# A two-block decoder stack on one Trainium2 core: shared keys projected once, rotary keys beside the latents, the merge in another order

## The reference, cut to what matters

```python
q = q_a.reshape(B, S, G, HPG, dh).transpose(0, 2, 3, 1, 4)          # G = 2 groups, HPG = 4 heads
k_cmp, v_cmp, k_slc, v_slc, k_win, v_win = [z.reshape(B, S, G, dh) for z in jnp.split(kv_a, 6, axis=-1)]
kc = _compress(k_cmp, pe_k, ck_w1, ck_w2)                           # blocks of 32 tokens, stride 16
vc = _compress(v_cmp, pe_v, cv_w1, cv_w2)
...
o_a = _nsa(q_a, kv_a, g_a, ...)      # compressed, selected and window attention, gated per head
o_b = _swa_sink(q_b, k_b, v_b, ...)  # window of 128, 2 groups, a sink
o_c = _fox(q_c, k_c, v_c, f_c, b_f)  # 8 heads with keys of their own, forgetting
merged = g[:, :, 0] * (o_a @ w_br_a) + g[:, :, 1] * (o_b @ w_br_b) + g[:, :, 2] * (o_c @ w_br_c)
return merged @ w_out
```

```python
c_q, c_kv, k_r, hq, hf, hi, hgate, mq, gate_logits = split_sizes(u @ w_in[l], IN_SPLITS)
k_rope = apply_rope(k_r, cos, sin)   # 32 wide, one for all 8 heads
ckv = rmsnorm(c_kv, kv_norm_g)
```

## Time and profile before

| | us |
|---|---|
| median of 3 runs | 2781.98 |
| lowest, highest | 2779.66, 2785.36 |
| the profiled execution, its own time | 2779.37 |
| its span from first to last instruction | 2777.3 |
| TensorE matmuls busy | 2729.1 (98%) |
| GpSimd busy | 2068.5 (74%) |
| ACT busy | 1300.9 (47%) |
| DVE busy | 857.4 (31%) |
| mean granted TensorE clock | 0.997 |

### The profile page before, as it was taken

One profiled execution on the slowest core, in us unless ns is written; L12 is line 12 of the kernel. 1 busy time (PEld: TensorE's weight loads), 2 busy tenths in 40 slices (PEclk: granted clock), 3 DMA queues, 4 the chain that ended last, 5 costly groups with the idle time before them and its releaser, 6 DMA issues. The chain is left out here.

```text
span 2777.3 us, 46964 instructions
## 1 busy us (share of the span) xinstructions
PE 2729.1 (98%) x19086; PEld 2516.8 (91%) x19086; DVE 857.4 (31%) x1473; ACT 1300.9 (47%) x1882; POOL 2068.5 (74%) x920
## 2 busy tenths in 40 slices
PE   8999999999999999999999999999999999999998
PEld 6999899899899989989899899988989989999898
DVE  2633264112224144311211323632121132263212
ACT  4454555444444555444444444644444444464443
POOL 7888566888988945788798774378879877437886
PEclk9999999999999999999999999999999999999999
DMA  6556533555665643755565554255556555425554
GB/s 229 183 190 210 169 122 130 196 184 181 211 191 185 202 150 115 189 191 189 174 208 184 174 177 158 84 176 188 189 167 211 189 169 181 160 84 175 181 185 143
DMA packets 131325, 484.13 MB, mean 174 GB/s; under 512 B 14720, under 2 KB 14720, under 8 KB 130112
## 3 DMA queue, kind: packets, MB, share of 16 engines
q1 hardware_dynamic: 127296, 463.53, 50.2%
q0 software_dynamic: 3840, 17.81, 2.2%
HBM read 478.65 MB, written 2.62 MB: 173 GB/s over the span
## 5 line engine op out<-in xcount | busy, mean ns | idle before, releaser
L1005 POOL TENSOR_TENSOR rest<-ring,upper 128x1024 fp32r<-128x1024 f32 (+2 forms) x848 | 2028.6, 2412 | 639.6 <-ACT upper L1775 620.7
L1775 ACT ACTIVATE upper<-ring 128x1024 fp32r<-128x1024 f32 (+2 forms) x848 | 884.0, 1052 | 775.0 <-DMA ring<-in_weights 773.5
L362 PE MATMUL psA<-xT_upper,upper 128*128 128x256 f32 x2944 | 411.1, 282 | 2.2 <-ACT arena L1775 2.2
L362 PE MATMUL psA<-xT_rest,upper 128*128 128x256 f32 x2944 | 413.1, 283 | 0.0
L362 PE MATMUL psA<-xT_upper,rest 128*128 128x256 f32 x2944 | 405.5, 280 | 0.0
L362 PEld LDWEIGHTS psA<-xT_upper,upper 128*128 128x128 f32 x2944 | 384.3, 189 | 16.0 <-ACT arena L1775 3.5
L362 PEld LDWEIGHTS psA<-xT_rest,upper 128*128 128x128 f32 x2944 | 379.7, 192 | 0.0
L362 PEld LDWEIGHTS psA<-xT_upper,rest 128*128 128x128 f32 x2944 | 372.8, 189 | 0.0
L1245 DVE TENSOR_TENSOR psA<-sil,psA 128x256 f32<-128x256 f32 x144 | 61.8, 429 | 954.3 <-ACT sil L1775 954.2
L362 PE MATMUL psY<-upper,hT_rest 128*128 128x512 f32 x704 | 205.3, 397 | 0.0
L362 PE MATMUL psY<-upper,hT_upper 128*128 128x512 f32 x704 | 203.8, 394 | 0.0
(11 more groups left out here) (258 smaller groups left out, 3185.8 us busy)
## 6 DMA issues: line engine op xcount, KB each, us to landing
ring<-in_weights SPq DMA_DIRECT2D x880, 512.0 KB, 3.3
G<-in_rows POOLq DMA_DIRECT2D x6, 1024.0 KB, 6.5
G<-in_rows POOLq DMA_DIRECT2D x7, 512.0 KB, 6.4
arena<-rel_by_distance POOLq DMA_DIRECT2D x8, 256.0 KB, 13.1
x<-in_x SPq DMA_DIRECT2D x2, 512.0 KB, 5.8
par<-in_params POOLq DMA_DIRECT2D x4, 256.0 KB, 5.8
xn<-in_mem POOLq DMA_DIRECT2D x1, 1024.0 KB, 9.6
memory_transposed<-arena POOLq DMA_DIRECT2D x1, 1024.0 KB, 5.8
```

What stands on the lines that cost most here:

```text
L362: i = pe.matmul(out, lhsT, rhs, start=start, stop=stop)
L1005: pool.tensor_tensor(rest[:, r, 0:n], ring[:, r, 0:n], upper[:, r, 0:n], ALU.subtract)\
L1775: act.activation(out, in_, func, **kw).then_inc(*up)
```

## The change

**Block 2's shared keys.** Heads are renumbered so that a pair of neighbours has one head of each group (`by_pairs` on the weights of `qa`, `qb`, the small gates, sinks, bias tables and branch outputs). Heads on partitions 0 to 63 are then of group 0 and those on 64 to 127 of group 1, and keys need not be doubled. `ks` and `kw` share one bank, `kc` and `vc` another, `kb` takes half a bank: five pieces and not ten. `Z2` gets its two halves by four copies for `k` and four for `v`, all out of the one bank. The two empty pieces are gone too: 213 pieces.

**Block 1's rotary keys.** They stand behind the latents as 64 more columns (704). DVE copies them out of banks Y2 and Y3, doubled, into `rotary`; ACT's squares of those banks wait for that; TensorE turns them into T0 after `mq`. 218 pieces.

**The merge.** `MERGE` gives a new order of the twelve products: (0,0), (0,1), (1,0), (0,2), (1,1), (1,2) and then as before. The third goes to bank Y2. The first is issued before the merge, in block 2 inside step 14 of attention, in block 1 behind attention. The last branch is turned before the third product. ACT splits further ahead around that place.

```diff
-PIECES = 220
+PIECES = (218, 213)
...
-WIDTHS = [_FFN + [PIECE] * 8 + [640] * 8 + [PIECE] * 26 + [0] * 6 + [PIECE] * 40 + _FFN,
-          _FFN + [PIECE] * 22 + [960] * 4 + [PIECE] * 8 + [0, PIECE] * 8 + [PIECE] * 16 + [0] * 2 + [PIECE] * 20 + _FFN]
+WIDTHS = [_FFN + [PIECE] * 8 + [704] * 8 + [PIECE] * 24 + [0] * 6 + [PIECE] * 40 + _FFN,
+          _FFN + [PIECE] * 17 + [960] * 4 + [PIECE] * 8 + [0, PIECE] * 8 + [PIECE] * 36 + _FFN]
...
+MERGE = [(0, 0), (0, 1), (1, 0), (0, 2), (1, 1), (1, 2)] + [(n, br) for n in range(2, 4) for br in range(3)]
...
+            def branch_product(i):
+
+                n, br = MERGE[i]
+                if n == 0:
+                    for t in range(TT):
+                        pe.wait_ge(*taken(("ot", BRANCHES[second()][br], t)))
+                s = shaped(piece(), PIECE, "p (k c) -> p k c", k=4)
+                lab = ("wo", br, n)
+                out = fill(pe, ("A0", "A1", "Y2")[i] if i < 3 else next_a(), lab)
...
             def merge(norm):
 
...
+                last = BRANCHES[second()][2]
+                for i in range(1, 12):
+                    if i == 2:
+                        turn_o(last, lambda qt: taken(("o", last, 0 if last == "mem" else 1, qt)))
+                    branch_product(i)
...
-                by_features("kr", 1)
                 by_features("mq", 2)
+                pe.wait_ge(*sig["rotary copied"].after(1))
+                turn("T0", ("kr", 0), [rotary[:, t, 64 * z:64 * z + P] for z in range(2) for t in range(TT)])
...
-                for n in ("ks", "kw", "kc", "vc"):
-                    by_features(n, 1)
+                by_features("ks kw", 1)
+                by_features("kc vc", 1)
                 by_features("qb", 2)
-                by_features("kb", 1)
+                lab = ("kb", 0)
+                s = shaped(piece(), PIECE, "p (k c) -> p k c", k=KD)
+                by_parts(fill(pe, next_a(), lab)[:, 0:S], s, filled(lab))
+                free()
...
-                           12: lambda: turn_o("swa", lambda qt: taken(("o", "swa", 1, qt)))}, opening)
-                for _ in range(2):
-                    piece()
-                    free()
+                           12: lambda: turn_o("swa", lambda qt: taken(("o", "swa", 1, qt))),
+                           14: lambda: branch_product(0)}, opening)
                 merge(norm + 2)
...
+                for t in range(TT):
+                    lab = ("c", 2 + t)
+                    dve.wait_ge(*full(lab))
+                    dve.tensor_copy(rotary[:, t, 64:192].rearrange("p (z d c) -> p z d c", z=2, d=2),
+                                    at(lab)[:, 256:320].rearrange("p (z c) -> p z c", z=2).unsqueeze(2)
+                                    .broadcast_to([P, 2, 2, 32])).then_inc(*sig["rotary copied"].up(t))
...
+                def pairs_of(at_column, ready):
+
+                    lab = ("kc vc", 0)
+                    dve.wait_ge(*ready)
+                    src = at(lab)[:, at_column:at_column + S]
+                    for g in range(2):
+                        v = src[64 * g:64 * g + 64]
+                        dve.tensor_copy(Z2[0:64, g, :], v).then_inc(*sig["vector step"].up())
+                        i = dve.tensor_copy(Z2[64:128, g, 0:S - 1], v[:, 1:S])
+                        i.then_inc(*(read(lab) if at_column and g else sig["vector step"].up()))
...
+                kept(("ks kw", 0), KSW)
+                pairs_of(0, full(("kc vc", 0)))
+                own()
+                blocks_of("k", par[:, 24:40])
+                pairs_of(S, sig["blocks"].after("k"))
+                dve.wait_ge(*full(("kb", 0)))
+                dve.tensor_copy(KB, at(("kb", 0))[:, 0:S]).then_inc(*read(("kb", 0)))
...
+def by_pairs(w, n):
+
+    return w.reshape(-1, 2, 4, n).transpose(0, 2, 1, 3).reshape(-1, 8 * n)
```

More of the change, by code:

```diff
@@ L305, in base, with pieces_here, after_mix @@
         def base():
-            return layer() * PIECES
+            n = layer()
+            return min(n, DEPTH) * PIECES[0] + max(n - DEPTH, 0) * PIECES[1]
+        def pieces_here():
+            return PIECES[second()]
+        def after_mix():
+            return pieces_here() - FFN_PIECES
         def steps_here():
@@ L659, in turn_o @@
                     turn(f"T{qt}", ("ot", name, qt), [O[:, qt, j * P:(j + 1) * P] for j in range(4)], ready(qt))
-            def merge(norm):
[L663 to L678, removed]
-                        free()
+            def branch_product(i):
[6 more added lines that the diff above has]
+                out = fill(pe, ("A0", "A1", "Y2")[i] if i < 3 else next_a(), lab)
+                for j in range(2):
+                    for w, v, first, last in passes():
+                        for k in range(4):
+                            mm(out[:, j * S:(j + 1) * S], s[w][:, k, j * P:(j + 1) * P], turned_parts[v][:, br, k],
+                               first and k == 0, last and k == 3, filled(lab) if last and j == 1 and k == 3 else None)
+                free()
+            def merge(norm):
+                last = BRANCHES[second()][2]
[3 more added lines that the diff above has]
+                    branch_product(i)
                 y = ("y", norm)
@@ new lines, in merge @@
+                added = {}
+                for n, br in MERGE:
+                    lab = ("wo", br, n)
+                    dve.wait_ge(*full(lab))
+                    src = at(lab).rearrange("p (j c) -> p j c", j=2)
+                    g = G[:, 8 * br + 2 * n:8 * br + 2 * n + 2, :]
+                    if br == 0:
+                        dve.wait_ge(*(taken(("ot", BRANCHES[second()][2], n)) if n < 2 else sig["merged parts"].after(n - 2)))
+                        stt_(sums_of(n), g, 1.0, src, ALU.add, ALU.mult).then_inc(*read(lab))
+                        if n > 1:
+                            rest_of(n - 1)
+                        continue
+                    tmp = (sil[:, :, :], xn[:, 0, 0:512].rearrange("p (a b) -> p a b", a=2))[br - 1]
+                    stt_(tmp, g, 1.0, src, ALU.add, ALU.mult).then_inc(*read(lab))
+                    dve.wait_ge(*taken(("wo", 0, n)))
+                    dve.wait_ge(*taken(lab))
+                    if br == 2:
+                        dve.wait_ge(*sig["vector step"].value(added[n]))
+                        tt_(sums_of(n), tmp, sums_of(n), ALU.add).then_inc(*sig["merged"].up(n))
+                    else:
+                        tt_(sums_of(n), tmp, sums_of(n), ALU.add).then_inc(*sig["vector step"].up())
+                        added[n] = sig["vector step"].count
+                    if (n, br) == (1, 1):
+                        rest_of(0)
@@ L1700, in block2 @@
                 dve.wait_ge(*full(("cmp", "k", 1)))
-                for g in range(2):
-                    zz = Z2[:, g, :]
-                    src = bass.AP(zz.tensor, zz.offset, [zz.ap[0], (2, 16), (16, 15)])
-                    i = tt_(ZB[:, :, 15 * g:15 * g + 15], src, par[:, 40:56].unsqueeze(2).broadcast_to([P, 16, 15]), ALU.add)
-                    i.then_inc(*(sig["blocks"].up("v") if g else sig["vector step"].up()))
+                dve.wait_ge(*taken(("kc vc", 0)))
+                blocks_of("v", par[:, 40:56])
                 lab = ("cmp out", "k")
@@ L2074, in block2 @@
                 for n in range(2):
-                    copy(("qf", n), QF[:, 2 * n:2 * n + 2, :], piece=93 + 2 * n)
-                until(99)
+                    copy(("qf", n), QF[:, 2 * n:2 * n + 2, :], piece=88 + 2 * n)
+                until(94)
                 for z in ("k", "v"):
```

174 lines of the change are left out of this document (69 added, 105 removed).

## The result

The changed kernel takes 2749.25 us (median of 4 runs, 2746.73 to 2751.27) against 2782.53 (4 runs beside it). The ratio is 0.987, with a 95% interval of 0.985 to 0.989. The forecast was 2746, with a range of 2738 to 2755. The profiled execution took 2751.27 us, 28.1 less than that of before; the forecast on that scale was 34.7 less.

A forecast was written before the change was run, and what follows sets the result against it. TensorE's own matmuls were taken to bound the kernel nearly everywhere. Removed matmuls, small additions, new and shortened waits summed to -34.7 us, 2747.3 against the 2782.0 median; the forecast was 2746, range 2738 to 2755.

The forecast's parts named there:

- Bound and price: Nearly everywhere TensorE's own matmuls set the end; a 256-column matmul costs 118.9 ns, a weight piece 2.85 us.
- rival that needed GpSimd or the ring as a bound: Shortened sections: GpSimd bounds next, 2752, chance 0.07; a wait for the ring in the projections would disprove the forecast.
- Rotary keys: Block 1: `kr` pieces gone, -11.4 us; wider latents +2.7, four added transposes a layer +0.8, all for two layers.
- The wait at A1: Block 2's `kc vc` bank: TensorE waits for vector-engine copies and additions, +4.8 us for two layers, bounds 0 to +8.1.
- Rival A: Block 2's `kc vc` bank: additions find GpSimd idle, the bank is free in time, no wait; 2741, chance 0.10.
- Rival C: Block 2's bank A1: the wait is long in both layers and the clock falls at both; 2753, chance 0.10.
- The `kb` bank: Block 2's projections: the copy TensorE waits for shrinks from 512 to 256 columns, -0.5 us in all.
- The merge: End of block 2's attention: the first branch product fills the 1.28 us `PT` wait, -2.6 us in all.
- the two new waits: Block 2, A1: waits of some 2.4 us may each bring a clock dip, +0 to +3.4 us, carried in the range.
- block 1's new order: Block 1's merge: no TensorE wait there today, so worth nothing and costing 0, at most +0.5 us a layer.
- Rivals D and E: Block 2: early product's piece comes late, 2753, chance 0.04; clock stays low after A1's wait, up to 2828, chance 0.01.
- The flag of 20 us at 0.5: Whole run: the forecast is wrong if the granted clock is at 0.5 for over 20 us in all.

The follow-up runs named there:

- e1: The changed kernel again with no edit, for another profile: 2747.47 us (6 runs), ratio 0.987.
- e2: The changed kernel with the old merge order, no early product and block 2's two unread pieces back: 2752.74 us (6 runs), ratio 0.989.
- e3: The kernel before with only the new merge, the two unread pieces gone: 2777.10 us (12 runs), ratio 0.997.
- e8: The changed kernel with block 2's first branch product behind attention, not in step 14, new order kept: 2755.27 us (6 runs), ratio 0.9885.
- e10: The kernel before with no edit, one more execution for another profile: 2795.05 us, mean granted clock 0.991.

## Why the prediction was right, point by point

- **Bound and price.** TensorE's list of matmuls set the time, and 2.85 us a piece held in every profile with the clock at full speed. 14 pieces gave 39.9 us less as worked out; no rival that needed GpSimd or the ring as a bound came up.
- **Rotary keys.** -10.7 and +2.6 us against -10.6 and +2.7. Nothing waits for the copies or the transposes. ACT's squares were covered as said. But the term had no place for the waits of block 1 that come with this part, for `hT_rest` and for `rest` in the second merge: some 1.8 and 0.9 us by the comparison of profiles under e1.
- **The wait at A1.** Right mechanism, right place, right bounds; the term was mis-sized, 2.4 in this profile and 2.0 in the mean where the sum had 4.8. Rival A, no wait at all, had 0.10 and is what two of the seven profiles showed in both layers. Rival C's fall of the clock behind the wait came in two of fourteen layers.
- **The `kb` bank.** 1.05 to 0.72 us a layer, -0.7 against -0.5.
- **The merge.** The `PT` hole closed as said, -3.0 against -2.6. But the term was mis-sized: by the times of e2, e3 and e8 the new merge is worth 5 to 8 us. The step that failed is the one that priced the hole of 1.28 us at its length alone. I carried the clock only for the two new waits, and did not ask what this wait does to it today: in 5 of 12 cases it is followed by 10.2 us at 0.5. The one profile of before that I had showed full speed there, and its own time was below the median. That block 1's new order costs nothing is not contradicted: its wait for `rest` is there with the old order too.
- **Rivals D and E.** The early product's piece was there in time: TensorE starts it at 1792.98, 0.36 us after the start of the transposes ahead of it, and the longest low stretch in any profile of the changed kernel was 6.8 us outside the program's end.
- **The flag of 20 us at 0.5.** It was set without counting the kernel before, whose own profile has 20.5 us of it (with the 6.8 us at the very end, where TensorE has nothing to do) and 53.8 in e10. The changed kernel had 34.8, 25.1 and 27.3 in three profiles. By its words it spoke against a forecast that came out; as a sign it was worthless.
- **The total.** 2749.25 in the first job and 2747.3 over all 16 runs against 2746. Over all runs the change is 36.5 us (2783.8 to 2747.3) where the sum had 34.7. The terms of the matmuls were sound. The others were off both ways, by estimates from the profiles: the wait at A1 2.8 us too dear, the clock 2.2 and the `PT` and `kb` waits 0.6 better than the sum had them; against that the norm behind block 2's mixer 2.1, `hT_rest` 1.8 and `rest` in block 1 0.9 us, which no term had. Together that makes 35.5. So the total is so near because errors cancelled, and that is luck.

## What to carry to other kernels

A hole in a saturated TensorE can cost more than its length: a wait of 1.28 us was followed by 10.2 us at clock 0.5 in 5 of 12 cases, at 4.3 us each, and with an independent product in the hole in none of 16. Read more than one profile of the kernel before if its runs spread by more than the effect you price, and look at the granted clock of each. When a bank has to wait for two uses of one buffer, take it out of the alternation: two free banks were worth 8 us here, where the waits in their rows were 3.4 and some 3 more were clock by estimate.

## What was not expected of the hardware

- Two executions of one program differ by 9 us (2749.5 and 2740.3 us of span). Most of it is the phase of GpSimd's 2.4 us subtractions against short vector operations, and the low clock behind the waits that follow: an operation of 0.17 us took 2.3, a pair of additions 1.4 to 5.2, the 1024-wide norm operation 1.28 or 2.8 to 3.0.
- The clock can fall behind a wait of 1.28 us, and a merge start at 0.5 shows the same busy share of TensorE as one at full speed, 9.4 of 10.2 us. Only the granted clock and the spacing of starts tell them apart.
- One lagging DMA engine of 16 takes a 512 KB load from 3.3 to 4.5 us and a 1 MB load beside it from 5 to 9, and keeps doing so over many loads.
